# Decay differences of a Mamba-2 scan on GpSimd instead of ScalarE, and the gates of z one step earlier

## The chip, the cores and the metric

The kernel runs on one NeuronCore of a Trainium2 chip, as one launch. The core has a matrix engine (TensorE, PE in the profile), a vector engine (VectorE, DVE), a scalar engine for activation functions (ScalarE, ACT), a general engine (GpSimd, POOL), a queue engine (SyncE, SP) and 16 DMA engines. Each engine works through its own list in order; semaphores tie the lists together. The metric is the time of one execution on the device in microseconds, as the median of several runs: 1495.35 us for three runs of the kernel before (1494.41 to 1498.49).

## What is computed

Two residual layers over 256 tokens of width 1024, all in float32: sliding-window attention with a dense SwiGLU, then a Mamba-2 mixer with a top-2-of-8 expert SwiGLU. The change is in the mixer. Cut to what matters there:

```python
z, xbc, dt = jnp.split(h @ w_in, [D_INNER, D_INNER + D_XBC], axis=-1)
xbc = jax.nn.silu(causal_depthwise_conv(xbc, conv_w, conv_b))
# ssd_chunked_scan: 2 chunks of 128 tokens, 4 groups of 8 heads
a_cs = jnp.cumsum((dt * a).reshape(b, nc, L, G, HG), axis=2)
decay = jnp.exp(jnp.where(causal, a_t[..., :, None] - a_t[..., None, :], -jnp.inf))
cb = jnp.einsum('bclgn,bcsgn->bcgls', cc, bc)
y_diag = jnp.einsum('bcghls,bcsghp->bclghp', cb[:, :, :, None] * decay, xd)
# states carried from chunk to chunk give y_off
y = y_diag + y_off + d_skip * xs
y = rms_norm(y * jax.nn.silu(z), norm_w)
return y @ w_out
```

`decay` is 128 x 128 for each of 32 heads and 2 chunks. The kernel computes the exponential of the difference clipped at zero, min(a_l - a_s, 0), so that nothing overflows above the diagonal; the mask comes with `cb`.

## The kernel before

Weights come from HBM in tiles of 128 x 1024. Each is split into a high part (`w_hi`, ScalarE, L1038) and a low part (`w_lo`, VectorE, L1581), and TensorE makes three products with high and low parts of the activations (L2685, L2686, L2693). Four buffers hold split tiles, so ScalarE and VectorE can be at most four tiles ahead of TensorE.

The mixer's input projection is 40 such tiles, called steps 0 to 39 here, in ten column groups: B, C, then x (groups 2 to 5), then the four groups of z (6 to 9), which end at steps 27, 31, 35 and 39. The output projection follows with 16 tiles. At each step every engine's code calls its own `mixer_steps(i)`, in which the remaining work of the mixer is placed at fixed steps: which step and in which order within it is written out by hand, and this is the order in that engine's list. Beside the projection run the convolution (`convolve` on VectorE, 8 instructions each, L2305 and L2308; its gate `conv_silu` on ScalarE, L1475) and the scan.

The scan has eight units u = 0 to 7, one for each pair of group and chunk. Unit u's parts stand at these steps:

- GpSimd (L2635 to L2639) fetches `acs_in`: the running sums of eight heads, spread over all partitions. The next fetch waits until the differences of this unit are done (`acs_used`).
- ScalarE, `unit_decays` (L1477 to L1495), at step 24 + 2u: eight differences 128 x 128 into `dec` (two buffers by u % 2), then one exponential 128 x 1024. From unit 2 on it waits first for TensorE's products of unit u - 2 (`acc_full`), which read the same buffer.
- VectorE, `unit_in` and `unit_mid` (L2368 to L2388), at step 24 + 2u: x times dt into `xd`; for chunk 0 also `xde` with `end_e`; then `dec` times the masked product `cbm` (L2376).
- TensorE, `unit_out`, at step 25 + 2u: one product with the state and eight with `dec` (L3330 or L3333, L3335).
- VectorE, `unit_out` (L2396 to L2405), at step 28 + 2u: adds them up.

ScalarE's `z_of_group(j)` (L1398 to L1406) applies SiLU to a finished z group, its two token halves one after the other. It stands two steps behind the group's last tile: steps 29, 33, 37 and 41. TensorE's first tile of the next z group uses the same accumulators and waits for it. `gated_by_z` on VectorE (L2416) multiplies with the result. ScalarE loads a function table (ACT_TABLE_LOAD) when the next function isn't in the one loaded: SiLU and Exp are in different ones, while copies, squares and Relu need no load.

After the mixer come a norm, the routing and the experts' tiles.

## Time and profile before

| what | value |
|---|---|
| median of three runs | 1495.35 us (1494.41 to 1498.49) |
| the profiled execution | 1497.73 us |
| its span, first to last instruction | 1495.9 us |
| mean granted TensorE clock | 0.991 |
| TensorE busy | 1437.1 us (96%) |
| VectorE busy | 995.1 us (67%) |
| ScalarE busy | 747.6 us (50%) |
| GpSimd busy | 18.6 us (1%), 27 instructions |
| scan: ScalarE's differences, first to last start | 487.6 to 557.6 us |
| output projection | 573.0 to about 619.5 us |

The profile is of one execution. Busy shares are averages over stages with different limits, so the stage around the change is read by itself: which engine waits there, for whom, and who would be next. PEclk is the clock that TensorE was granted as a share of 2.4 GHz; half of it is its lower level. Instructions overlap a little at their ends, so two starts lie closer than one duration.

### The profile page before, as it was taken

Reading aid. Unit: us, or ns where it says so; the run is one execution under the profiler, and the core shown is the slowest. Engines: PE = TensorE matmul, PEld = TensorE weight load, DVE = VectorE, ACT = ScalarE, POOL = GpSimd, SP = SyncE. Lnnn points to the kernel's source line nnn. Section 1 sums busy time; section 2 is a strip of 40 time slices with the busy share of each in tenths; the row PEclk is TensorE's granted clock in tenths of the full one; section 3 lists DMA queues with packets and bytes.
Section 4 is the critical chain, followed back from the end, with each engine's and each line's share of the span. In section 5 each row is a group of like instructions: output and inputs, shape, how many; then the busy total and the mean of one; then the engine's idle time right before and its main releaser. Section 6 shows DMA issues by size and latency. Waiting matters only on the chain.

```text
span 1495.9 us, 18527 instructions
## 1 busy us (share of the span) xinstructions
PE 1437.1 (96%) x6840; PEld 976.6 (65%) x6840; DVE 995.1 (67%) x1271; ACT 747.6 (50%) x977; POOL 18.6 (1%) x27
## 2 busy tenths in 40 slices
PE   7989999999999899999999999999999989999998
PEld 2835787888789778674666556756465655565573
DVE  2578788888659899764666646765654555655563
ACT  3565544444455896353446445644453444545361
POOL 0000000000000000000100000000000000000000
PEclk9999999999999999999999999999999999999999
DMA  9878698888366545679999999999999999999996
GB/s 361 330 248 292 240 396 303 301 295 301 103 217 185 162 161 204 261 288 409 364 412 406 411 374 416 418 420 420 409 420 413 420 420 418 413 420 414 420 419 247
DMA packets 118201, 506.01 MB, mean 338 GB/s; under 512 B 13779, under 2 KB 16492, under 8 KB 83032
## 3 DMA queue, kind: packets, MB, share of 16 engines
q1 hardware_dynamic: 115640, 496.51, 85.6%
q0 software_dynamic: 2464, 8.24, 1.6%
q8 instruction: 57, 0.93, 0.2%
q14 instruction: 40, 0.33, 0.1%
HBM read 502.52 MB, written 2.32 MB: 337 GB/s over the span
## 4 chain that ended last, share of the span: by engine, by line
PE 74%; DVE 10%; DMA 7%; ACT 6%; issue 3%; SPq 0%; DVEq 0%; ACTq 0%
PE acc L2685 16%; PE acc L2693 16%; PE acc L2686 16%; PE acc L3187 15%; DVE w_lo L1581 3%; ACT w_hi L1038 2%; DVE cv L2308 2%; DMA raw_rest<-in_moe_w_down 1%; DMA raw<-in_moe_w_down 1%; PE xb L3071 1%; DMA mod<-in_moe_w_gu 1%; PE acc L2834 1%; DMA mod<-in_moe_w_down 1%; DMA raw<-in_ada_w 1%; ACT dec L1487 1%
## 5 line engine op out<-in xcount | busy, mean ns | idle before, releaser
L1581 DVE TENSOR_TENSOR w_lo<-raw,w_hi 128x1024 fp32r<-128x1024 f32 x356 | 427.3, 1221 | 136.6 <-ACT w_hi L1038 126.1
L1038 ACT ACTIVATE w_hi<-raw 128x1024 fp32r<-128x1024 f32 x356 | 371.0, 1057 | 249.1 <-PE acc L2693 157.7
L2685 PE MATMUL acc<-w_hi,g_hi 128*128 128x512 f32 x448 | 179.3, 400 | 4.0 <-ACT w_hi L1038 3.9
L2686 PE MATMUL acc<-w_hi,g_lo 128*128 128x512 f32 x448 | 174.8, 390 | 0.0
L2685 PE MATMUL acc<-w_hi,a_hi 128*128 128x512 f32 x384 | 155.4, 405 | 8.5 <-ACT z_s L1404 7.7
L2686 PE MATMUL acc<-w_hi,a_lo 128*128 128x512 f32 x384 | 151.4, 394 | 0.0
L2693 PE MATMUL acc<-w_lo,g_hi 128*128 128x512 f32 x448 | 139.1, 392 | 4.1 <-DVE w_lo L1581 4.1
L3187 PE MATMUL acc<-raw,g_s 128*64 128x512 f32 x592 | 131.6, 594 | 0.5 <-DMA raw<-in_moe_w_gu 0.5
L2693 PE MATMUL acc<-w_lo,a_hi 128*128 128x512 f32 x384 | 119.5, 392 | 0.0
L1581 DVE TENSOR_TENSOR w_lo<-mod,w_hi 128x1024 fp32r<-128x1024 f32 x66 | 78.5, 1221 | 60.0 <-ACT w_hi L1038 58.2
L2685 PEld LDWEIGHTS acc<-w_hi,g_hi 128*128 128x128 f32 x448 | 84.2, 188 | 38.4 <-issue 12.7
L1038 ACT ACTIVATE w_hi<-mod 128x1024 fp32r<-128x1024 f32 x66 | 68.1, 1056 | 63.4 <-PE acc L2693 24.6
L2693 PEld LDWEIGHTS acc<-w_lo,g_hi 128*128 128x128 f32 x448 | 83.4, 188 | 24.9 <-DVE w_lo L1581 7.1
L3187 PEld LDWEIGHTS acc<-raw,g_s 128*64 128x64 f32 x592 | 41.3, 137 | 82.5 <-issue 77.8
L2686 PEld LDWEIGHTS acc<-w_hi,g_lo 128*128 128x128 f32 x448 | 84.2, 188 | 16.2
L2685 PEld LDWEIGHTS acc<-w_hi,a_hi 128*128 128x128 f32 x384 | 73.1, 190 | 27.5 <-ACT z_s L1404 8.1
L2685 PE MATMUL acc<-w_hi,e_hi 128*128 128x512 f32 x216 | 87.8, 406 | 2.5 <-issue 2.1
L2686 PE MATMUL acc<-w_hi,e_lo 128*128 128x512 f32 x216 | 85.3, 395 | 0.0
L2693 PEld LDWEIGHTS acc<-w_lo,a_hi 128*128 128x128 f32 x384 | 72.9, 190 | 16.0
L2686 PEld LDWEIGHTS acc<-w_hi,a_lo 128*128 128x128 f32 x384 | 73.2, 191 | 14.0
L2693 PE MATMUL acc<-w_lo,e_hi 128*128 128x512 f32 x216 | 68.6, 399 | 5.8 <-DVE w_lo L1581 5.7
L1618 DVE SCALAR_TENSOR_TENSOR ada<-raw,cond,ada 128x512 f32<-128x512 f32 x84 | 59.1, 746 | 1.4 <-DMA raw<-in_ada_w 1.4
(417 smaller groups left out, 2057.3 us busy)
## 6 DMA issues: line engine op xcount, KB each, us to landing
raw<-in_moe_w_gu SPq DMA_DIRECT2D x136, 1024.0 KB, 14.8
raw<-in_moe_w_down SPq DMA_DIRECT2D x66, 1024.0 KB, 16.5
raw<-in_ada_w SPq DMA_DIRECT2D x96, 512.0 KB, 6.0
mod<-in_moe_w_gu SPq DMA_DIRECT2D x40, 1024.0 KB, 13.8
raw<-in_ffn_w_gu SPq DMA_DIRECT2D x56, 512.0 KB, 5.9
mod<-in_moe_w_down SPq DMA_DIRECT2D x23, 1024.0 KB, 16.3
raw_more<-in_moe_w_gu SPq DMA_DIRECT2D x22, 1024.0 KB, 14.3
raw<-in_ssm_w_in SPq DMA_DIRECT2D x40, 512.0 KB, 5.0
```

The lines of the kernel that those rows point to most:

```text
L1038: act.activation(w_hi[:, w % SPLIT, :], raw_tile(no), ACT.Copy).then_inc(hi_ready, 1)
L1487: ins = act.activation(dec[:, u % 2, cols], acs_in[:, cols], ACT.Relu, scale=-1.0, bias=acs[:, c, HG * g + i:HG * g + i + 1])
L1581: dve.tensor_tensor(w_lo[:, w % SPLIT, :], raw_tile(no), r32(w_hi[:, w % SPLIT, :]), ALU.subtract).then_inc(raw_used, 1)
L1618: ins = dve.scalar_tensor_tensor(dst, src, cond[:, k:k + 1], dst, ALU.mult, ALU.add)
L2308: ins = dve.scalar_tensor_tensor(cv[:, s % 2, m, :], src, wt, cv[:, s % 2, m, :], ALU.mult, ALU.add)
L2685: pe.matmul(o, l_hi[:, k, rows_], hi[:, col:col + HALF], start=new, stop=False)
L2686: pe.matmul(o, l_lo[:, k, rows_], hi[:, col:col + HALF], start=False, stop=False)
L2693: mm = pe.matmul(o, l_hi[:, k, rows_], lo[:, col:col + HALF], start=False, stop=end)
L2834: mm = pe.matmul(o[j:j + 32, 0:HALF], cond[:, k:k + 1].to_broadcast([P, 32]), raw_tile(no)[:, cols], start=k == 1, stop=k >= KD - 2, skip_ ...
L3071: mm = pe.transpose(b[:, m * P:(m + 1) * P], hidden[:, block_of(m)] if B.mixture else hidden[:, m * P:(m + 1) * P], ident)
L3187: mm = pe.matmul(rows_[at_:at_ + SMALL, :], lhs[:, k, :], raw_tile(no)[:, m * HALF:(m + 1) * HALF], start=k == 0, stop=last, skip_group_ch ...
```

## The change

The differences leave ScalarE. GpSimd computes them itself, directly behind the transfer that brings `acs_in`, with one subtract-and-min instruction a head; it now waits for the running sums (unit 0), for the products of unit u - 2, and for its own transfer. ScalarE keeps the exponential, whose sign changes with the clipped difference, and in unit 0 the exponential of the chunk ends comes ahead of it. ScalarE's gates of z stand one step earlier and ahead of the exponential in their step.

```diff
@@ ScalarE, mixer_steps
                 if i not in DECAYS_FIRST:
                     conv_silu(i)
+                for j in range(SG):
+                    if i == PROJ_END[Z0 + j] + 1:
+                        z_of_group(j)
                 for u in range(NU):
                     if i == unit_in_at(u) + LEAD:
                         unit_decays(u)
                 if i in DECAYS_FIRST:
                     conv_silu(i)
-                for j in range(SG):
-                    if i == PROJ_END[Z0 + j] + 2:
-                        z_of_group(j)
@@ ScalarE, unit_decays
                 if u == 0:
                     act.wait_ge(acs_ready, 1)
-                if u >= 2:
-                    act.wait_ge(acc_full, full_no(u - 2))
-                act.wait_ge(ld_acs, 16 * (u + 1))
-                for i in range(HG):
-                    cols = slice(i * P, (i + 1) * P)
-                    ins = act.activation(dec[:, u % 2, cols], acs_in[:, cols], ACT.Relu, scale=-1.0,
-                                         bias=acs[:, c, HG * g + i:HG * g + i + 1])
-                ins.then_inc(acs_used, 1)
+                    act.activation(end_e[:, :, :], end_e[:, :, :], ACT.Exp).then_inc(acse_ready, 1)
                 act.wait_ge(acs_used, u + 1)
-                if u == 0:
-                    act.activation(end_e[:, :, :], end_e[:, :, :], ACT.Exp).then_inc(acse_ready, 1)
-                act.activation(dec[:, u % 2, :], dec[:, u % 2, :], ACT.Exp, scale=-1.0).then_inc(e_ready, 1)
+                act.activation(dec[:, u % 2, :], dec[:, u % 2, :], ACT.Exp).then_inc(e_ready, 1)
@@ GpSimd, for u, (c, g) in enumerate(SUNITS), behind the transfer
+                if u == 0:
+                    pool.wait_ge(acs_ready, 1)
+                if u >= 2:
+                    pool.wait_ge(acc_full, full_no(u - 2))
+                pool.wait_ge(ld_acs, 16 * (u + 1))
+                for i in range(HG):
+                    cols = slice(i * P, (i + 1) * P)
+                    ins = pool.tensor_scalar(dec[:, u % 2, cols], acs_in[:, cols], acs[:, c, HG * g + i:HG * g + i + 1], 0.0,
+                                             ALU.subtract, ALU.min)
+                ins.then_inc(acs_used, 1)
```

ScalarE's list in step 28, between the convolution's gate (L1475) and the exponential of unit 2 (L1493 before, L1484 now), with what follows it in the list before:

```order
 L1475 ACTIVATE cv<-cv 128x512
-L1487 ACTIVATE dec<-acs_in,acs 128x128 x8
-L1493 ACT_TABLE_LOAD
-L1493 ACTIVATE dec<-dec 128x1024
-L1038 ACTIVATE w_hi<-raw 128x1024
-L1431 ACTIVATE xbc<-xb 128x2x256
+L1404 ACTIVATE z_s<-acc 128x512
+L1406 ACTIVATE z_s<-acc 128x512
+L1484 ACT_TABLE_LOAD
+L1484 ACTIVATE dec<-dec 128x1024
```

The eight differences are gone, and the two halves of the gate of z group 0 stand where they stood, behind the gate that uses the same table.

GpSimd's list before, from the store of the running sums to the store of hm, with the semaphores waited for:

```order
L2633 DMA acs_scratch<-dt_rows 32x2x128 [waits acs_rows]
L2638 DMA acs_in<-acs_scratch 128x1024 [waits st_acs]
L2638 DMA acs_in<-acs_scratch 128x1024 [waits acs_used] x7
L2642 DMA hm_scratch<-hm 128x2x1024 [waits hm_rows,hm_rest]
L2595 DMA token_scratch<-token_rows,slot_at 1536x16 [waits token_ready,place_ready,st_zero,st_hm]
```

And now, for units 1 and 2:

```order
L2629 DMA acs_in<-acs_scratch 128x1024 [waits acs_used]
L2638 TENSOR_SCALAR dec<-acs_in,acs 128x128 [waits ld_acs]
L2638 TENSOR_SCALAR dec<-acs_in,acs 128x128 x7
L2629 DMA acs_in<-acs_scratch 128x1024 [waits acs_used]
L2638 TENSOR_SCALAR dec<-acs_in,acs 128x128 [waits ld_acs,acc_full]
```

Each transfer is followed by the unit's differences, and the next transfer stands behind them.

## Rows read from the trace of the kernel before

**Rows 1.** Busy time by stretch: us, busy us (count) of each engine, PEclk, DMA share, GB/s.
```profile
460.00:470.00 10.00, 10.00 (x86) 10.00 (x85) 9.40 (x20) 5.17 (x7) 0.00 (x0) 1.00 0.72 204
...
505.00:515.00 10.00, 4.40 (x27) 3.47 (x25) 8.67 (x15) 8.28 (x15) 0.53 (x1) 0.91 0.44 152
515.00:525.00 10.00, 9.60 (x36) 7.53 (x36) 9.30 (x17) 8.58 (x17) 0.53 (x1) 0.74 0.50 159
...
580.00:600.00 20.00, 20.00 (x97) 16.69 (x96) 19.93 (x23) 10.13 (x13) 0.00 (x0) 1.00 0.76 305
...
620.00:630.00 10.00, 8.51 (x51) 5.37 (x49) 8.96 (x17) 5.28 (x11) 0.00 (x0) 1.00 0.00 0
...
1300.00:1400.00 100.00, 100.00 (x458) 63.44 (x458) 58.77 (x60) 51.09 (x55) 0.00 (x0) 1.00 1.02 417
```

**Rows 2.** Waits, 485 to 580 us: who waited for whom, total us, times, longest.
```profile
PE acc L2685 <- ACT z_s L1404: 7.7, 2, 6.0
```

**Rows 3.** TensorE's timeline: start, us, engine, line, operation, count, [idle before].
```profile
498.40 1.89 PE L3335 MATMUL acc<-xd,dec 128*128 128x64 f32 x16
...
505.92 0.62 PE L2693 MATMUL acc<-w_lo,a_hi 128*128 128x512 f32 x2
...
508.96 0.44 PE L3322 MATMUL xb<-c_t,b_t 128*128 128x128 f32 x2
515.40 0.80 PE L2685 MATMUL acc<-w_hi,a_hi 128*128 128x512 f32 x1 [6.00 <-ACT z_s L1404]
...
520.42 0.60 PE L2733 MATMUL xb<-square,cv 128*128 128x128 f32 x4
520.78 0.48 PE L2685 MATMUL acc<-w_hi,a_hi 128*128 128x512 f32 x1
...
523.61 1.02 PE L3330 MATMUL acc<-xde,xbc 128*128 128x512 f32 x2
...
547.76 0.61 PE L2693 MATMUL acc<-w_lo,a_hi 128*128 128x512 f32 x2
...
554.34 0.80 PE L2685 MATMUL acc<-w_hi,a_hi 128*128 128x512 f32 x1 [1.73 <-ACT z_s L1404]
...
558.74 0.60 PE L2733 MATMUL xb<-square,xbc 128*128 128x128 f32 x4
...
573.00 0.48 PE L2685 MATMUL acc<-w_hi,y_hi 128*128 128x512 f32 x1
```

**Rows 4.** VectorE: its timeline, then three groups of 500 to 572 us.
```profile
491.71 0.69 DVE L2384 TENSOR_TENSOR xde<-xd,end_e 128x512 f32<-128x512 f32 x1 [2.33 <-ACT end_e L1492]
...
512.11 1.23 DVE L2388 TENSOR_TENSOR dec<-dec,cbm 128x1024 f32<-128x1024 f32 x1 [0.70 <-ACT dec L1493]
...
545.11 1.22 DVE L1581 TENSOR_TENSOR w_lo<-raw,w_hi 128x1024 fp32r<-128x1024 f32 x1
...
569.50 0.69 DVE L1645 TENSOR_TENSOR y_lo<-xb,y_hi 128x512 fp32r<-128x512 f32 x1
...
L1581 DVE TENSOR_TENSOR w_lo<-raw,w_hi 128x1024 fp32r<-128x1024 f32 x15 | 18.3, 1219 | 0.9 <-ACT w_hi L1038 0.6
...
L2405 DVE TENSOR_TENSOR xbc<-xbc,acc 128x512 f32<-128x512 f32 x7 | 4.8, 686 | 0.2
...
L2376 DVE TENSOR_TENSOR cbm<-xb,square 128x128 f32<-128x128 f32 x6 | 1.7, 288 | 0.6 <-DVE cv L2308 0.6
```

**Rows 5.** ScalarE's timeline around step 28.
```profile
507.20 2.44 ACT L1487 ACTIVATE dec<-acs_in,acs 128x128 f32<-128x128 f32 x8
509.66 1.28 ACT L1493 ACT_TABLE_LOAD   x1
510.95 1.06 ACT L1493 ACTIVATE dec<-dec 128x1024 f32<-128x1024 f32 x1
...
514.75 0.60 ACT L1404 ACTIVATE z_s<-acc 128x512 f32<-128x512 f32 x1
```

**Rows 6.** GpSimd: its timeline, and the transfers of acs_in.
```profile
0.26 0.10 POOL L3457 MEMSET const-float32-0.0<- 128x1 f32 x1 [0.26 <-issue]
...
DMA to landing us min/median/max: 4.1/4.4/5.3
```

## The prediction

> **What bounds the kernel now.** I read the chain that ended last first, then the busy time by stretch, then the timelines of the scan. From about 760 us to the end the transfers run without a gap (DMA share 1.02 at 417 GB/s) while TensorE is nearly always busy [rows 1]: that part cannot shrink, but it starts when the part in front lets it. At 620 to 630 us nothing is moved at all, so there the engines set the time and not the transfers [rows 1]. A microsecond won or lost in the scan should therefore arrive at the end, unless something takes it on the way.
>
> In the scan (484 to 582 us) TensorE waits in one place worth naming: for ScalarE's gates of z, 7.7 us in two waits [rows 2]. The first tile of z group 1 (step 28) could start at 508.96 + 0.44 = 509.40 and starts at 515.40; the first of group 3 (step 36) starts at 554.34 after 1.73 us [rows 3]. Both tiles then run long: 515.40 to 520.42 is 5.02 us, 554.34 to 558.74 is 4.40, against 520.78 to 523.61 = 2.83 for an undisturbed tile [rows 3]. In that stretch the granted clock averages 0.91 and later 0.74 of 2.4 GHz, that is, the engine fell to its lower level after standing idle [rows 1]. So the two waits cost 6.00 + 2.19 + 1.73 + 1.57 = 11.5 us. The next candidate stands right behind: VectorE is 9.30 of 10 us busy at 515 to 525, in the middle of a disturbed stretch, and 19.93 of 20 at 580 to 600 [rows 1]. The 0.70 us before its instruction at 512.11 are its last wait for another engine that counts [rows 4].
>
> **The removed instructions on ScalarE.** Eight differences take 2.44 us per unit [rows 5], eight units: 19.5 us leave ScalarE's list. Two table loads of 1.28 us come back (the moved gate now stands between a state or convolution gate and an exponential, and in the new order there are 12 loads where there were 10). Net some 17 us of an engine that isn't itself the bound; what counts is what it lets go sooner.
>
> **The z gate.** Before, the gates of group 0 stand behind the differences, a table load, the exponential, a split and a copy: from 507.20 to 514.75 [rows 5]. Now they stand directly behind the convolution's gate in step 28. They then wait only for step 27's tile, whose last two products start at 505.92 and take 0.62 [rows 3]. The first half is out by then; the second takes 0.6 more [rows 5]: 507.1, ahead of 509.40. The wait of 6.00 us goes, and with it the slow clock: up to 8.2 us at step 28. For group 3 the same working puts the gates ahead of TensorE as well.
>
> **What is late next: VectorE.** It can only come forward by its own waits. The two large ones are 2.33 us for the exponential of the chunk ends (now ahead of everything, because the differences in front of it are gone) and 0.70 for the exponential of unit 2 [rows 4]. The last limits the sum: exponential 2 stands behind the z gates, 507.1 + 1.28 (table) + 1.06 = 509.4, against 512.0 now [rows 5]. VectorE's product of unit 2 moves from 512.11 to about 509.5 [rows 4]: 2.6 us earlier, and all behind it by the same, since it runs solid. TensorE can use only that plus the lead that VectorE has over it. The leads: at step 35 the low part is out at 545.11 + 1.22 = 546.33 and is wanted at 547.76, 1.43 us; at the start of the output projection y_lo is out at 569.50 + 0.69 = 570.19 and is wanted at 573.00, 2.81 us [rows 3, 4]. At step 35 TensorE can be 1.43 + 2.6 = 4.0 us early; the second z wait and its slow clock (3.3 us) lie behind it, so this gives 7.3 at step 40; there y_lo allows 2.81 + 2.6 = 5.4. The last number is the ceiling: **5.4 us**, not 11.5.
>
> **The added work on GpSimd.** It issues eight differences per unit behind each transfer, and holds the next transfer until they are done; nothing else is queued there but hm's store, wanted after 620. Transfers land in 4.4 us [rows 6]. For unit u it waits for the products of unit u-2: for unit 2 these start at 498.40 and take 1.89 [rows 3], so it has from 500.3 to about 508.4 before ScalarE's exponential stands still. For units 5 and 7 the time allowed is 11.7 and 9.7 us, for unit 3 10.4 (each: VectorE's product at its new time, less 1.06 for the exponential, less the end of the products two units back). What one GpSimd difference takes no row shows. Lower end: the 128x1 memset, 0.10 us. Upper end of the nearest kind: ScalarE's same difference, 2.44 / 8 = 0.305, and VectorE's 128x128 product, 0.288 [rows 4 to 6]. Eight at 0.305 are 2.4 us: hidden everywhere.
>
> **What GpSimd takes from VectorE.** This is the term that decides. Of the 72 us from 500 to 572, VectorE works some 70, and only about 14 of them lie in the seven groups that read PSUM or one tensor; the rest read two tensors from SBUF (one group of either kind is shown, with the 128x128 product) [rows 4]. If a GpSimd instruction that reads SBUF holds off a VectorE one, 48 of them (units 2 to 7) fall into the stretch where VectorE is solid, some 80% = 38 against such a reader. The price of one collision lies between 0 and 0.305 us: 0 to 11.6 us in all. I take 0.11, near the memset's length, the only compute row of this engine: VectorE has small gaps of its own (some 0.2 us, as behind each convolution) where a read can hide. 38 x 0.11 = 4.2 us. Units 0 and 1 fall to 457 to 470 us, where TensorE is solid and VectorE 9.40 of 10 busy [rows 1]: I cost them at nothing; uncovered they would be 16 x 0.11 = 1.8 us.
>
> **The sum.** -5.4 + 4.2 = -1.2 us. The profiled execution took 1497.73 (span 1495.9 and 1.8 around it), 2.4 above the median of the three runs, 1495.35; so it would come to 1496.5 and the median to **1494.1 us**.
>
> **The rivals.**
> *The port is free.* VectorE loses nothing: -5.4, 1490.0 us. For it: the differences are short, and nothing in this profile shows GpSimd disturbing VectorE. Against: it never computed here. 27%.
> *GpSimd holds VectorE off for its whole length.* The place is VectorE's list from 500 to 570, the price 0.305 x 38 = 11.6, the result +6.2: 1501.5 us. It turns the change into a loss from 5.4 / 38 = 0.14 us per collision. For it: VectorE's work there is four fifths two-tensor reads. Against: the gaps. 25%. The Trainium skill ("SBUF — State Buffer", who interferes with whom) states just such a rule: a VectorE instruction with two SBUF inputs and a GpSimd one that reads SBUF exclude each other, and the second to issue blocks fully. No run here shows it yet. For the price, the skill ("GPSIMD Engine Reference", performance versus the Vector engine) gives 1.8 cycles an element at 1.2 GHz, an estimate of 0.19 us for 128 elements; by that the sum would be -5.4 + 7.2 = +1.8 us.
> *GpSimd itself is too slow.* From 9.7 us per unit (1.2 us an instruction, which could also come from being held off by VectorE) ScalarE waits for the differences, and behind it the splits. At 1.6 us an instruction (12.8 us a unit) it is some 3 us over for units 3, 5 and 7: +9 - 5.4 = +3.6, 1499.0 us. 8%.
> *The gain doesn't arrive.* The transfers of the expert part swallow it: 0, 1495.3 us. Against: 620 to 630 us without any transfer. 8%.
> My forecast itself: 32%.
>
> **Range and chances.** 0.3% is 4.5 us, about what a measurement of this kernel tells from no change. Faster by more needs a free port and little lost to short waits (a short stall can itself bring the slow clock, as 1.73 us did at step 36): most of the first rival, 28% with the edge of the forecast. Slower by more: most of the second and third, 29%. Between: 43%. The range leaves out the tail beyond 0.2 us per collision and a half: 1489.0 to 1502.5 us.
>
> **What the profile of the changed kernel would show.** That the z step is right: no TensorE wait for z_s above 1 us, granted clock near 1 at 505 to 525. That VectorE is next: TensorE waits for w_lo at steps 31 to 35 and for y_lo at the start of the output projection. The port: VectorE's 128x1024 subtractions longer than 1.22 us, or pauses before them, only while GpSimd works; if they stay at 1.22 the first rival holds. GpSimd's speed: the distance between starts of its differences. If the exponential of units 3 to 7 waits for dec from GpSimd, the third rival holds. I am wrong if the wait for z stays, if TensorE is over 5.4 us early at the first tile of the output projection, or if the shift there isn't the shift at the end.

## The result and the profile after

| | median | runs | profiled execution, its span |
|---|---|---|---|
| before | 1495.95 us | 1494.41 to 1498.49 (4) | 1497.73, 1495.9 us |
| changed | 1504.2 us | 1502.42 to 1506.05 (4) | 1502.42, 1500.6 us |

The ratio is 1.0054, 95% interval 1.0034 to 1.0073: slower, by 8 us in the medians, and outside the range of the prediction. (The two profiled executions lie only 4.7 us apart: that of before is one of its slower runs, that of the changed kernel its fastest.) The first tile of the output projection starts at 578.49 instead of 573.00, 5.5 us late, so the loss is made in the scan.

The waits of the scan come first, since [rows 2] had its answer there. From 485 to 590 us (engine, line, waited for: us in total, times, longest):

```profile
ACT dec L1484 <- POOL dec L2638: 22.8, 6, 8.2
POOL dec L2638 <- DMA acs_in<-acs_scratch: 16.6, 5, 3.5
...
DVE dec L2379 <- ACT dec L1484: 7.6, 5, 2.5
...
PE xb L2734 <- ACT xbc L1431: 6.3, 2, 4.0
```

The wait for z is gone. In its place stands a chain: TensorE's transposition (`xb<-square,cv`) waits for ScalarE's copy of x (`xbc`), VectorE for ScalarE's exponential, ScalarE for GpSimd's differences (22.8 us in six waits), GpSimd for its transfer. GpSimd's timeline shows why:

```profile
499.56 8.31 POOL L2638 TENSOR_SCALAR dec<-acs_in,acs 128x128 f32<-128x128 f32 x8 [18.66 <-PE acc L3336]
508.17 0.58 POOL L2629 DMA_DIRECT2D acs_in<-acs_scratch  x1 [0.30 <-POOL dec L2638]
511.92 7.84 POOL L2638 TENSOR_SCALAR dec<-acs_in,acs 128x128 f32<-128x128 f32 x8 [3.17 <-DMA acs_in<-acs_scratch]
...
560.81 7.66 POOL L2638 TENSOR_SCALAR dec<-acs_in,acs 128x128 f32<-128x128 f32 x8 [3.18 <-DMA acs_in<-acs_scratch]
```

In units 2 to 7 eight differences take 7.66 to 8.56 us, about 1.0 us each, not 0.3. Then 0.30 us to the issue, 0.58 for it, 3.2 to 3.5 until the data are there, and only then the next eight: there is one `acs_in`. From unit 2 to unit 7 the starts lie (560.81 - 499.56) / 5 = 12.25 us apart. TensorE needs much less. Where it doesn't wait (e5 below), its products of one unit and the next start at

```profile
516.77 1.89 PE L3341 MATMUL acc<-xd,dec 128*128 128x64 f32 x16
...
525.58 1.89 PE L3341 MATMUL acc<-xd,dec 128*128 128x64 f32 x16
```

8.8 us apart. GpSimd falls behind by 3.4 us a unit. ScalarE's timeline of the changed kernel, answering [rows 5]:

```profile
504.70 0.58 ACT L1404 ACTIVATE z_s<-acc 128x512 f32<-128x512 f32 x1
505.70 0.60 ACT L1406 ACTIVATE z_s<-acc 128x512 f32<-128x512 f32 x1 [0.43 <-PE acc L2694]
506.32 1.28 ACT L1484 ACT_TABLE_LOAD   x1
507.90 1.06 ACT L1484 ACTIVATE dec<-dec 128x1024 f32<-128x1024 f32 x1 [0.30 <-POOL dec L2638]
...
519.79 1.06 ACT L1484 ACTIVATE dec<-dec 128x1024 f32<-128x1024 f32 x1 [3.06 <-POOL dec L2638]
520.75 1.04 ACT L1038 ACTIVATE w_hi<-raw 128x1024 fp32r<-128x1024 f32 x1
521.70 0.58 ACT L1431 ACTIVATE xbc<-xb 128x512 f32<-128x512 f32 x1
```

In step 28 all is as forecast: the second half of z is out at 506.3 and the exponential 3.05 us sooner than in [rows 5]. Of these, 0.87 us are from ahead of the scan, whose first product starts at 484.09 in this execution and at 484.96 in that of before; the change itself gives 2.2. One unit later the exponential waits, and the split and the copy of x behind it wait too. TensorE's timeline, answering [rows 3], shows who needed them:

```profile
522.42 0.71 PE L2734 MATMUL xb<-square,cv 128*128 128x128 f32 x4 [2.31 <-ACT xbc L1431]
536.98 1.09 PE L2734 MATMUL xb<-square,cv 128*128 128x128 f32 x4 [3.95 <-ACT xbc L1431]
...
559.46 0.50 PE L2686 MATMUL acc<-w_hi,a_hi 128*128 128x512 f32 x1 [2.33 <-ACT w_hi L1038]
...
578.49 0.47 PE L2686 MATMUL acc<-w_hi,y_hi 128*128 128x512 f32 x1 [1.10 <-DVE y_lo L1636]
```

And by stretch, with the columns of [rows 1]:

```profile
505.00:515.00 10.00, 10.00 (x53) 8.05 (x53) 9.48 (x16) 7.08 (x9) 6.54 (x8) 1.00 0.45 157
515.00:525.00 10.00, 7.68 (x40) 6.29 (x39) 8.86 (x14) 6.37 (x10) 6.29 (x8) 0.89 0.32 110
...
535.00:545.00 10.00, 8.02 (x39) 6.74 (x40) 7.31 (x9) 4.29 (x7) 8.56 (x8) 0.83 0.33 111
```

The stretch of the old z wait is full now (10.00 busy, clock 1.00, against 4.40 and 0.91). The loss lies behind it, where every engine but GpSimd stands: VectorE, 9.50 busy before at 535 to 545, has 7.31.

The lengths of VectorE's own instructions hardly suffer. The group from 485 to 572 us that lost most in total (mean ns of one behind the comma), before and then changed:

```profile
L2308 DVE SCALAR_TENSOR_TENSOR cv<-u_pad,vecs,cv 128x256 f32<-128x256 f32 x18 | 7.4, 478 | 0.0
```

```profile
L2299 DVE SCALAR_TENSOR_TENSOR cv<-u_pad,vecs,cv 128x256 f32<-128x256 f32 x18 | 8.0, 509 | 0.0
```

This group, `xbc<-xbc,srow` (684 and then 745 ns) and the five groups with smaller differences (`w_lo`, the other convolution, `raw` and the two scalings, 9 to 41 ns a piece) come to 1.6 us over 48 instructions of GpSimd, 0.03 us each. VectorE's own loss is in its waits for the exponential, 7.6 us in the list above.

### The profile page after: what moved, and what is told of

Same layout as the page of the kernel before. It is cut to its first block, busy times and chain, and to the rows that moved or that the text cites. A ratio compares the mean times of both kernels' runs of the same rounds, so it can differ in the third digit from the quotient of the medians.

```text
span 1500.6 us, 18531 instructions
## 1 busy us (share of the span) xinstructions
PE 1436.4 (96%) x6840; PEld 974.1 (65%) x6840; DVE 996.8 (66%) x1271; ACT 731.3 (49%) x915; POOL 84.6 (6%) x91
## 4 chain that ended last, share of the span: by engine, by line
PE 76%; DMA 9%; DVE 7%; POOL 3%; ACT 3%; issue 2%; SPq 0%; DVEq 0%; ACTq 0%; POOLq 0%
PE acc L2686 16%; PE acc L2694 16%; PE acc L2687 15%; PE acc L3188 15%; POOL dec L2638 3%; DVE w_lo L1572 3%; DMA raw_rest<-in_moe_w_down 1%; DMA mod<-in_moe_w_gu 1%; DMA raw<-in_moe_w_down 1%; PE xb L3072 1%; DMA acs_in<-acs_scratch 1%; PE acc L2835 1%; DMA raw<-in_moe_w_gu 1%; ACT w_hi L1038 1%; DMA mod<-in_moe_w_down 1%
## 5 line engine op out<-in xcount | busy, mean ns | idle before, releaser
L2638 POOL TENSOR_SCALAR dec<-acs_in,acs 128x128 f32<-128x128 f32 x64 | 65.6, 1040 | 44.7 <-DMA acs_in<-acs_scratch 26.0
```

The costliest lines, as they stand in the source:

```text
L2638: ins = pool.tensor_scalar(dec[:, u % 2, cols], acs_in[:, cols], acs[:, c, HG * g + i:HG * g + i + 1], 0.0, ALU.subtract, ALU.min)
```

## The experiments

Theory 1 at the start: GpSimd's loop is too slow. Its rivals: the early z gates cost by themselves, or GpSimd's work costs VectorE time. The medians, and, as the yardstick in the trace, the way from TensorE's first product of unit 0 (`xb<-c_t,b_t` near 484 us) to the first tile of the output projection. The way is one execution each and free of what varies ahead of the scan; before and e4, whose lists are the same up to there, both have 88.04.

| kernel | median us | ratio, 95% interval | way us |
|---|---|---|---|
| before | 1495 to 1496.8 | 1 | 88.04 |
| changed | 1504.2 | 1.0054 [1.0034, 1.0073] | 94.40 |
| e1 z gates early, all on ScalarE | 1500.21 | 1.0037 [1.0023, 1.0050] | 91.80 |
| e2 GpSimd alone, z as before | 1505.43 | 1.0072 [1.0058, 1.0086] | 97.39 |
| e3 changed, two buffers | 1495.1 | 0.9995 [0.9986, 1.0004] | 86.56 |
| e4 before, with a probe on GpSimd | 1496.77, one run | | 88.04 |
| e5 differences ahead of conv gate | 1491.03 | 0.9969 [0.9959, 0.9980] | 83.74 |
| e6 e5, z group 0 early | 1492.66 | 0.9977 [0.9967, 0.9986] | 84.06 |
| e7 e6, even units on GpSimd | 1499.23 | 1.0030 [1.0016, 1.0044] | 89.87 |
| e8 e5, all z gates early | 1495.6 | 1.0004 [0.9995, 1.0014] | 87.27 |
| e9 changed, in place | 1505.7 | 1.0066 [1.0041, 1.0092] | 95.90 |
| e10 e9, z nearly as before | 1505.51 | 1.0056 [1.0036, 1.0077] | 97.54 |
| e11 e5, z group 1 early | 1493.7 | 0.9981 [0.9971, 0.9991] | 85.03 |
| e12 e11, squares one step later | 1491.15 | 0.9968 [0.9955, 0.9982] | 82.34 |
| e13 e8, four of eight on GpSimd | 1494.6 | 0.9989 [0.9979, 0.9998] | 85.69 |
| e14 e12, four of eight on GpSimd | 1491.33 | 0.9970 [0.9957, 0.9982] | 83.56 |

### The two parts apart: e1 and e2

e1 is the kernel before with only this:

```diff
                 if i not in DECAYS_FIRST:
                     conv_silu(i)
+                for j in range(SG):
+                    if i == PROJ_END[Z0 + j] + 1:
+                        z_of_group(j)
...
-                for j in range(SG):
-                    if i == PROJ_END[Z0 + j] + 2:
-                        z_of_group(j)
```

> The kernel before with the z gates alone moved one step up; the differences stay on ScalarE. Theory A (GpSimd's loop of transfer, eight differences and next transfer, 12 us a unit through one buffer, is what cost the time; the z part is sound): the wait of 6.0 us for z at step 28 and the slow clock behind it go, but VectorE doesn't come forward, since the exponential of unit 2 still stands behind the differences. TensorE can then use only VectorE's leads, 1.4 us at step 35 and 2.8 at the first tile of the output projection: -2.8 us. Theory B (moving z in front of the exponentials delays the exponentials and with them VectorE): 0 to +2 us, and VectorE waits for exponentials after step 28.

Measured +5 us, above both theories. No wait for z is left, but its waits from 485 to 590 us are:

```profile
PE xb L2733 <- ACT xbc L1431: 8.1, 3, 3.8
...
DVE dec L2388 <- ACT dec L1493: 4.8, 4, 2.4
DVE w_lo L1581 <- ACT w_hi L1038: 3.3, 4, 2.2
```

So moving the z gates is a loss by itself: 7.7 us of waits for z turned into 8.1 us of waits for the copy of x, and VectorE waits more. What stands behind the gate now, the differences, a load, the exponential, a split, a copy, is what TensorE and VectorE need next. Theory B has the direction, and sees only VectorE in it.

e2 is the changed kernel with the z gates back at their old places (that diff reversed).

> The changed kernel with the z gates at their old place: only the differences move to GpSimd. Theory A (one buffer in series): GpSimd's starts stay 12 us apart for units 2 to 7, and the time is the changed kernel's or slightly above it, +8 to +11 us on before. Theory B (the z gates ahead of the exponential are what delays): near before, -2 to +2 us, and the starts on GpSimd are further apart only where the products come late.

```profile
ACT dec L1484 <- POOL dec L2638: 29.0, 6, 7.6
...
PE acc L2686 <- ACT z_s L1404: 14.8, 3, 6.5
```

Measured +10 us (1505.43 against 1495.05). ScalarE waits for GpSimd as in the changed kernel, and with z behind it TensorE waits for z three times and longer than ever. That is theory A. Each part alone loses, and they don't add up (5 and 10 against 8). With the differences on GpSimd the early gates cost nothing more: 1.2 us less in the median, where the intervals overlap, and 3.0 us less on the way. So the 5 us of e1 are no part of the changed kernel's 8.

### GpSimd's loop and its price: e3 and e4

e3 gives the transfers a second buffer, so that GpSimd fetches unit u + 2 while it works on u + 1:

```diff
+            fetch(0)
+            fetch(1)
             for u, (c, g) in enumerate(SUNITS):
...
-                pool.wait_ge(ld_acs, 16 * (u + 1))
+                pool.wait_ge(ld_two[u % 2], 16 * (u // 2 + 1))
...
+                if u + 2 < NU:
+                    pool.wait_ge(acs_used, u + 1)
+                    fetch(u + 2)
```

> The changed kernel with a second buffer for acs_in in a free slot of the modulation rows and one semaphore for each: the transfer of unit u + 2 runs under the differences of unit u + 1. Theory A (series of transfer and differences): the 4.1 us between the end of one unit's differences and the start of the next go, the eight differences alone are 8.3 us against 8.8 us for TensorE's pitch of a unit, ScalarE's waits for GpSimd shrink from 22.8 us to under 5, and the time is below before: -5.4 + about 2 for VectorE's lengthened instructions = -3 us. Theory C (the shared port: what costs is that VectorE and GpSimd hold each other off): VectorE's instructions and GpSimd's stay as long, and the time stays above before by at least 3 us.

```profile
499.42 9.28 POOL L2642 TENSOR_SCALAR dec<-acs_in,acs 128x128 f32<-128x128 f32 x8 [24.37 <-PE acc L3343]
...
509.62 9.15 POOL L2642 TENSOR_SCALAR dec<-acs_in_b,acs 128x128 f32<-128x128 f32 x8
...
551.13 9.36 POOL L2642 TENSOR_SCALAR dec<-acs_in_b,acs 128x128 f32<-128x128 f32 x8
```

The period falls to (551.13 - 499.42) / 5 = 10.3 us, and the time by 9 us: taking the transfer out of the series gives back what the changed kernel had lost against the kernel before. It gives no more. Theory A had expected 3 us below before and under 5 us of waits of ScalarE for GpSimd; the time is that of before, and the waits are 12.7 us in five. GpSimd pauses only once for TensorE, 0.86 us, and still misses 8.8: its eight take 8.0 to 11.2 us, 9.4 in the mean. Theory C's 3 us above before are ruled out too. In the same order of the z gates e3 is 5 us below e1 (1495.1 against 1500.21): there GpSimd's work, fetched ahead, is the better choice.

e4 is the kernel before, with like instructions of GpSimd put into two places (they write `dec`, which nobody reads by then; `flat` is `dec` as one row, `tri` a constant; a few more take a number instead of the column, one of them at 128x512): behind the scan, where VectorE is solid (it works without a pause), and at 611 us, where it waits.

```diff
+                for m in range(n):
+                    pool.tensor_scalar(flat[:, m * P:(m + 1) * P], tri, column[:, 5:6], 0.0, ALU.subtract, ALU.min)
...
+            pool.wait_ge(y_ready, NU)
+            probe(8, 2)
+            pool.wait_ge(token_ready, 1)
+            probe(4, 1)
```

> The kernel before; GpSimd additionally runs difference instructions on constants into the unused dec buffers: eight 128x128 with a scalar from memory, two 128x128 with an immediate scalar and one 128x512 with an immediate, once from about 579 us, where VectorE is solid, and four, one and one from about 612 us, where VectorE stands idle for 5.7 us. Theory C (the shared port makes GpSimd's instruction long): about 1.0 us each under the solid VectorE and 0.3 or less in the idle stretch. Theory D (the instruction itself costs GpSimd 1 us, whatever VectorE does): about 1.0 in both. The immediate forms and the 128x512 tell whether the cost is one of the instruction or of its elements.

```profile
578.12 14.69 POOL L2644 TENSOR_SCALAR dec<-square 128x128 f32<-128x128 f32 x8 [28.64 <-DVE xbc L2417]
592.88 2.39 POOL L2646 TENSOR_SCALAR dec<-square 128x128 f32<-128x128 f32 x2
...
611.67 2.79 POOL L2644 TENSOR_SCALAR dec<-square 128x128 f32<-128x128 f32 x4 [13.88 <-DVEq L2455]
614.53 0.64 POOL L2646 TENSOR_SCALAR dec<-square 128x128 f32<-128x128 f32 x1
615.24 1.92 POOL L2647 TENSOR_SCALAR dec<-square 128x512 f32<-128x512 f32 x1
```

One 128x128 instruction takes 2.79 / 4 = 0.70 us beside an idle VectorE and 14.69 / 8 = 1.84 us beside a solid one: neither theory C's 0.3 nor theory D's 1.0 in both places. ScalarE is idle in the fast place too, so e4 alone can't say which of the two engines holds GpSimd off. The transfers don't: their share is 1.03 in the fast place and 0.63 in the slow one. e13 below has four at 0.70 us beside a busy ScalarE (1.90 of 2.79 us), while three of VectorE's four instructions read or write `acc`, in PSUM:

```profile
515.55 2.79 POOL L2662 TENSOR_SCALAR dec<-acs_in,acs 128x128 f32<-128x128 f32 x4 [2.71 <-PE acc L3360]
```

That points to VectorE, and to its instructions with all inputs in SBUF, as far as one place can. VectorE, over the stretch with eleven of GpSimd's (ten of 128x128, one of 128x512), needs 18.60 us from one `w_lo` to a later one, for what takes 17.97 without: 0.06 each. But 0.40 of these 0.63 us are in one instruction, beside the 128x512 one, that takes 1.62 us instead of 1.22:

```profile
595.92 1.62 DVE L1582 TENSOR_TENSOR w_lo<-raw,w_hi 128x1024 fp32r<-128x1024 f32 x1
```

So beside ten short instructions of 128x128 GpSimd is held off and VectorE hardly at all (0.23 us, an estimate from the rest); beside the one long one VectorE is held off too.

### The order of ScalarE's list: e5, e6, e8, e11, e12

In the kernel before ScalarE stands 2.93, 2.44 and 0.79 us for the convolution with the differences right behind. The second, in step 28:

```profile
506.67 0.63 ACT L1475 ACTIVATE cv<-cv 128x512 f32<-128x512 f32 x1 [2.44 <-DVEq L2314]
```

e5 puts them in front, and leaves everything else as it was before:

```diff
+                for u in range(NU):
+                    if i == unit_in_at(u) + LEAD:
+                        unit_differences(u)
                 if i not in DECAYS_FIRST:
                     conv_silu(i)
```

> The kernel before with one change: in each step ScalarE does its eight differences ahead of the convolution's gate instead of behind it; the gates of z stay where they were, GpSimd does nothing new. Theory 1 (what decides is the order of ScalarE's list in step 28 and its neighbours, since ScalarE stands still for the convolution there, 2.4 and 0.8 us, while the differences could run): the exponential, the split and the z gate come up to 2.4 us sooner, the wait of TensorE for z at step 28 shrinks from 6.0 to about 3.5 us, and the time falls by 2 to 4 us: 1491 to 1493. Theory 2 (the differences wait for the products two units back and for their transfer, so ahead of the convolution's gate they only pass their wait on to it): VectorE's and TensorE's waits for the gate appear, the time is 1495 to 1498.

```profile
509.85 0.50 PE L2691 MATMUL acc<-w_hi,a_hi 128*128 128x512 f32 x1 [1.33 <-ACT z_s L1404]
531.16 0.79 PE L2691 MATMUL acc<-w_hi,a_hi 128*128 128x512 f32 x1 [3.41 <-ACT z_s L1404]
```

Faster by 4.6 us (0.9969), with no instruction added or removed, as theory 1 had it (1491 to 1493). The wait for z at step 28 falls from 6.00 to 1.33 us, more than the 2.4 expected; a new one of 3.41 comes at step 32.

e6 adds the early gate for z group 0 alone, e8 for all four groups:

> As the run before, and in addition the gates of z of group 0 alone one step up, in step 28 directly behind the convolution's gate (they share its table of functions, no load is added); groups 1 to 3 stay. Theory 1 (a z gate moved up is good where TensorE stands still for it for 6 us and where no load comes with it; moving all four groups cost 5 us because of what stands behind them): the wait of 6.0 us and the slow clock behind it go, the way from unit 0's first product to the output projection is 83 to 85 us instead of 88.0, the time 1490 to 1492. Theory 2 (any z gate in front of exponential, split and copy costs elsewhere what it gives here): TensorE waits 2 to 4 us for the copy of x or the split instead, the time is 1494 to 1498.

> The kernel before with the differences ahead of the convolution's gate, and the z gates of all four groups one step up; nothing on GpSimd. The z gates alone one step up took 1500.2 (+5 us). Theory 1 (they cost by what stands behind them: 2.4 us of differences are now in front of the gate instead, in ScalarE's idle time): TensorE's waits for the copy of x shrink from 8.1 us to about half, the time is 1495 to 1498. Theory 2 (they cost by the two added table loads and the lost lead of one step, whatever stands behind): 1499 to 1501, as without the move.

e6 loses the wait at step 28 and gets one of 1.28 us for `w_lo` and 3.97 for z at step 32: no gain over e5 (0.9977 against 0.9969). That is theory 2's claim, that such a gate costs elsewhere what it gives here; the time, 1492.66, lies between the ranges of the two. e8 is back at the time of before. Theory 1 of that run has its numbers: the time is in its range, and the waits for the copy of x are about halved, from 8.1 us in e1 to this one:

```profile
533.61 0.63 PE L2739 MATMUL xb<-square,cv 128*128 128x128 f32 x4 [3.90 <-ACT xbc L1431]
```

Its cause isn't borne out by that. In e5's order, too, the z gates all one step up cost 4.6 us, the same as in the old order (5 us): what e8 has over e1 is e5's own gain. So the differences behind the gates were not what made these dear.

e11 moves only group 1's gate, into step 32 behind the convolution's gate, and e12 also the squares:

```diff
-                    if i == PROJ_END[Z0 + j] + 2:
+                    if i == PROJ_END[Z0 + j] + 2 - (j == 1):
...
-                    if i == PROJ_END[Z0 + u // 2] + 4 + u % 2:
+                    if i == PROJ_END[Z0 + u // 2] + 4 + u % 2 + (u < 6):
```

> The kernel with the differences on ScalarE ahead of the convolution's gate (1491.0 us), and the z gate of group 1 one step sooner directly behind the convolution's gate. In that kernel TensorE stood 3.41 us for this gate at 527.75 to 531.16 and ran the next tile at the slow clock (5.25 us from its start to the next x piece). Theory 1: the wait shrinks by what now stands between the two places (a square, a split and a copy, 2.0 us) to 1.4 us, -2 to -4 us: 1487 to 1489. Theory 2 (what is put behind the gate, the split and the copy, is waited for in its place): 1490 to 1492.

> As the run before, and in addition the squares of y for units 0 to 5 one step later on ScalarE, since it stands 2.9, 2.7 and 2.4 us for them while differences behind them could run. Theory 1 (ScalarE's in-order waits are what delays its gates and splits): the wait for z of group 1 goes, VectorE or the split's low part is next, another -1 to -3 us: 1485 to 1488. Theory 2 (VectorE is the bound by now, 93% busy at 515 to 545): the same time as the run before within 1 us.

e11 missed both its ranges: 1493.7, its way 1.3 us longer than e5's. Its trace shows where. The wait of 3.41 us is down to 1.36, but the clock falls behind it all the same, and group 3's gate now makes TensorE wait:

```profile
528.84 0.50 PE L2691 MATMUL acc<-w_hi,a_hi 128*128 128x512 f32 x1 [1.36 <-ACT z_s L1404]
...
550.17 0.80 PE L2691 MATMUL acc<-w_hi,a_hi 128*128 128x512 f32 x1 [2.32 <-ACT z_s L1404]
```

The tiles behind the two take 4.46 and 4.40 us instead of 2.83, so waits and slow clock come to 6.9 us, against 3.41 and a tile of 5.25 us, 5.8 in all, in e5. That is 1.1 of the 1.3 us. e12 missed its ranges as well (1485 to 1488, or e11's time within 1 us): it is 2.5 us below e11. It has the shortest way of all, 82.34 us; its time can't be told from e5's. What bounds it then can be read from its waits and stretches:

```profile
532.67 0.73 PE L2699 MATMUL acc<-w_lo,a_hi 128*128 128x512 f32 x2 [1.19 <-DVE w_lo L1587]
542.12 0.73 PE L2699 MATMUL acc<-w_lo,a_hi 128*128 128x512 f32 x2 [0.84 <-DVE w_lo L1587]
...
566.03 0.47 PE L2691 MATMUL acc<-w_hi,y_hi 128*128 128x512 f32 x1 [1.01 <-DVE y_lo L1651]
```

```profile
525.00:535.00 10.00, 8.81 (x48) 7.02 (x47) 9.39 (x12) 9.97 (x21) 0.53 (x1) 1.00 0.38 127
```

VectorE is 9.3 to 9.5 of 10 busy from 505 to 555 us, and TensorE waits for it 2.5 us for `w_lo` and 1.0 for `y_lo`, at the places that the prediction named, with the clock at 1.00 (the columns of [rows 1]). One wait for z is left, 1.33 us at step 28. From 573.00 the first tile of the output projection comes to 566.03, and the span falls by 7.3 us with it: what is won in the scan arrives. (These are two executions; in the medians it is 4.8 us, the ratio 0.9968.)

### GpSimd with a shorter list: e7, e9, e10, e13, e14

e7 gives GpSimd only the even units (two buffers, e6's order):

```diff
+                if u % 2 == 0:
+                    return
...
-                act.wait_ge(ld_acs, 16 * (u + 1))
+                act.wait_ge(ld_two[1], 16 * (u // 2 + 1))
```

> As the run before, and in addition two buffers for the transfers, and the differences of units 0, 2, 4 and 6 on GpSimd, those of units 1, 3, 5 and 7 still on ScalarE. GpSimd has 17.6 us for each of its units then and needs 8 to 10, so by theory 1 (the added work was bad only by its serial loop) ScalarE waits for it under 1 us, loses 9.8 us of work, and the time is that of the run before or up to 2 us less: 1489 to 1491. By theory 2 (GpSimd's work costs by what it takes from VectorE, 32 instructions by 0.06 to 0.3 us) it is 2 to 8 us above the run before.

```profile
539.15 9.88 POOL L2660 TENSOR_SCALAR dec<-acs_in,acs 128x128 f32<-128x128 f32 x8 [4.39 <-PE acc L3361]
```

```profile
549.06 1.06 ACT L1503 ACTIVATE dec<-dec 128x1024 f32<-128x1024 f32 x1 [4.52 <-POOL dec L2660]
```

Half the work, and 6.6 us slower than e6. Theory 1 failed, since the period isn't all; the 6.6 us lie in theory 2's range, but its cause, time taken from VectorE, is not where the trace has the largest wait. GpSimd may start unit 6 only at 539.15, when the products of unit 4 have read `dec`; from there to the exponential it needs 9.9 us where ScalarE needs 2.4. Behind that exponential stands z's gate, and TensorE waits for it 5.01 us. So the length of the eight in a row counts too, once the way from one use of `dec` to the next is tight. (TensorE's waits for `w_lo` grow as well, from 1.3 to 2.6 us.)

e9 was to free GpSimd of that as well: differences in place in `acs_in`, two buffers, the exponential writes `dec`.

```diff
+                    ins = pool.tensor_scalar(acs_two[u % 2][:, cols], acs_two[u % 2][:, cols], acs[:, c, HG * g + i:HG * g + i + 1], 0.0,
+                                             ALU.subtract, ALU.min)
+                ins.then_inc(acs_used, 1)
+                if 1 <= u < NU - 1:
+                    pool.wait_ge(e_ready, u)
+                    fetch(u + 1)
```

> The changed kernel with GpSimd's loop opened: two buffers for the transfers, and the differences written in place in them instead of into dec, so that GpSimd waits for no product of TensorE and works up to two units ahead; ScalarE's exponential reads the buffer, writes dec and takes over the wait for the products two units back. The 64 differences on GpSimd and the order of the z gates stay as changed. Theory 1 (the changed kernel lost by the latency of GpSimd's loop: transfer, then differences of some 8 us, tied to the products two units back): ScalarE's wait for GpSimd goes, and the time falls from 1504 to 1490 to 1493, below the kernel before, since ScalarE is rid of 19.5 us of work. Theory 2 (the 64 instructions cost VectorE their length, and the early z gates cost by themselves as they did alone): 1497 to 1501, TensorE waiting for w_lo and for the copy of x.

> GpSimd's opened loop as in the run before, but the z gates at their old places, save that of group 1, which comes one step sooner directly behind the convolution's gate (same table of functions, no load added): 10 loads as before. Theory 1: without the differences ScalarE reaches every z gate 2.4 us sooner or more, so none of TensorE's waits for z above 1 us is left, VectorE bounds the scan: 1487 to 1490. Theory 2 (GpSimd's instructions cost VectorE): 2 to 5 us above the same order without GpSimd, that is 1491 to 1494.

```profile
509.23 9.07 POOL L2641 TENSOR_SCALAR acs_in_b<-acs_in_b,acs 128x128 f32<-128x128 f32 x8 [4.20 <-DMA acs_in_b<-acs_scratch]
518.25 0.59 POOL L2631 DMA_DIRECT2D acs_in<-acs_scratch  x1
523.11 8.00 POOL L2641 TENSOR_SCALAR acs_in<-acs_in,acs 128x128 f32<-128x128 f32 x8 [4.27 <-DMA acs_in<-acs_scratch]
```

The edit did not do what it was for. The fetch of unit u + 1 stands behind the differences of unit u in GpSimd's list, so transfer and differences are in series again, with a period of 13.1 us (e10: 13.2), and both kernels are as slow as the changed one or slower, outside the ranges of both theories. Unmeant, they extend the series over the period: 10.3, 12.2, 13.1 us give ways of 86.6, 94.4, 95.9 us in the same order of z.

That left open whether GpSimd's work costs anything once it keeps up. e13 (e8's order) and e14 (e12's order) share each unit: four differences on GpSimd, four on ScalarE, the exponential in two halves, two buffers.

```diff
-                for i in range(HG):
+                for i in range(HG // 2, HG):
                     cols = slice(i * P, (i + 1) * P)
...
-                act.activation(dec[:, u % 2, :], dec[:, u % 2, :], ACT.Exp, scale=-1.0).then_inc(e_ready, 1)
+                act.activation(dec[:, u % 2, HALF:2 * HALF], dec[:, u % 2, HALF:2 * HALF], ACT.Exp, scale=-1.0)
+                act.wait_ge(diffs_down, u + 1)
+                act.activation(dec[:, u % 2, 0:HALF], dec[:, u % 2, 0:HALF], ACT.Exp).then_inc(e_ready, 1)
```

> The z gates all one step up as in the changed kernel, two buffers for the transfers, and the eight differences of each unit shared: four on GpSimd, four on ScalarE ahead of the convolution's gate; the exponential in two halves. In the runs so far the starts of GpSimd's differences lay 12.2 us apart in the changed kernel, 13.1 and 13.2 in two variants whose transfer still stood behind the differences, and 10.3 with two buffers, and the times were 1504, 1506, 1506 and 1495. Theory 1 (GpSimd's period against TensorE's 8.8 us a unit is the whole loss): four differences take 4 to 5 us, GpSimd keeps up, ScalarE waits for it under 1 us in all, and the time is at or below the same order without GpSimd (1495.6): 1492 to 1495. Theory 2 (each instruction on GpSimd also costs VectorE): 32 instructions, 0.06 to 0.3 us each, 1497 to 1503.

> The best order so far (all differences on ScalarE ahead of the convolution's gate, the z gate of group 1 one step up, squares of y one step later: 1491.15 us) with the same sharing: four differences of each unit on GpSimd, four on ScalarE. Theory 1: GpSimd keeps up and disturbs little, but VectorE already bounds (TensorE waits 2.5 us for its low parts), so the time is the same within 1.5 us: 1490 to 1492.5. Theory 2: GpSimd's 32 instructions lengthen a VectorE that bounds: 1493 to 1500.

GpSimd now mostly waits for TensorE instead of the reverse. In e14:

```profile
517.05 5.11 POOL L2662 TENSOR_SCALAR dec<-acs_in,acs 128x128 f32<-128x128 f32 x4 [4.84 <-PE acc L3360]
```

e13 takes 1494.6 (0.9989) against 1495.6 (1.0004) of the same order without GpSimd, e14 1491.33 (0.9970) against 1491.15 (0.9968): the intervals overlap in both pairs, barely in the first. Both times are in the range of theory 1 and outside that of theory 2. But ScalarE still waits for GpSimd, once for 1.8 us in e13, where theory 1 allowed under 1, and three times in e14:

```profile
ACT dec L1502 <- POOL dec L2662: 7.3, 3, 3.5
```

The ways are 1.6 us shorter than e8's and 1.2 us longer than e12's. So the difference is at most a microsecond or two either way, and its sign isn't shown. What leaves ScalarE (9.8 us of differences, less 1.5 for the exponential in two halves) gains no more than that. In e14 VectorE bounds by then: TensorE waits 3.5 us for its `w_lo`, 2.5 in e12.

## Why the prediction was wrong

It said 1494.1 (1489.0 to 1502.5) and gave slower 29%; the time is 1504.2.

**The removed instructions and the z gate (its own view of step 28): right there.** The wait of 6.00 us and the slow clock went, the exponential of unit 2 came out 3.05 us sooner. 2.6 was forecast for VectorE; it has 509.07 against 512.11, of which 0.87 is from ahead of the scan, so 2.2.

**"Eight at 0.305 are 2.4 us: hidden everywhere": this step failed first.** The price came from the two engines whose like instructions the trace showed, and its upper end was 0.305 us. GpSimd needs 0.70 alone (e4), 0.96 to 1.07 in the changed kernel's units 2 to 7. The trace of before had no row of GpSimd computing, so the upper end was no bound at all: the nearest row belonged to another engine.

**The allowance was computed for the wrong thing.** The prediction says that the transfer is held until the differences are done and that it lands in 4.4 us, and then compares the differences alone with the 9.7 to 11.7 us between products and exponential. In series the loop is 0.3 + 0.6 + 3.3 + 8.0 = 12.2 us against 8.8 for a unit on TensorE. That condition breaks at (8.8 - 4.2) / 8 = 0.57 us an instruction, not at the 1.2 us that it gave. This is the point from which GpSimd is no longer hidden, not yet the one from which the change loses: e3 has a period of 10.3 us and the time of before. A cautious price, three times a neighbour's, gives 8 x 0.92 + 4.2 = 11.5 us, between e3's period and the changed kernel's: a loss of some microseconds. e3 shows the term: without the transfer in the loop 9 us come back.

**The third rival had the mechanism and only 8%.** It looked for 1.6 us an instruction and 1499.0 us; 1.0 us an instruction was enough for 1504.2, by the series above. Its sum is off as well: 12.8 us against the allowances that it gives itself, 10.4, 11.7 and 9.7, is 2.4 + 1.1 + 3.1 = 6.6 us over, not 9.

**The z gates as a pure gain: wrong.** The prediction worked out when z would be ready and what VectorE gains, and took the engines behind the gate as served. e1 measures +5 us for this part alone; beside GpSimd's work (changed kernel against e2) it gives 1.2 us within the noise, where up to 8.2 were forecast at step 28. Under "What is late next" the answer given was VectorE; it was ScalarE's own list, above all the copy of x that TensorE transposes (8.1 us of waits in e1, 6.3 in the changed kernel), and e8 finds the same 4.6 us in another order.

**What GpSimd takes from VectorE: mis-sized.** 0.11 us each were put in, 4.2 us in all; measured 0.03 (changed kernel) to 0.06 (e4, 0.02 without the long one). So the term of which the prediction says that it decides was some 1.6 us. The second rival had the direction reversed: VectorE holds GpSimd off, 1.84 us against 0.70. The rule of the Trainium skill ("SBUF — State Buffer", who interferes with whom), that the two exclude each other and the second to issue blocks, fits GpSimd's side; on VectorE's side these runs show it beside the one instruction of 128x512 (1.62 us against 1.22) and almost none of it beside those of 128x128.

**VectorE as the next bound, and the shift that arrives at the end: borne out, but in another kernel.** The changed kernel never got there. e12 did, with the differences on ScalarE and the squares moved: its way is 88.04 - 82.34 = 5.7 us shorter, TensorE waits for `w_lo` and `y_lo`, and it arrives in the time. That this is near the 5.4 us of the prediction is partly luck, since they were worked out for other lists; whether 5.4 would have been the changed kernel's ceiling no run shows.

What stays open: which part of e8's 4.6 us is the two added loads and which the lost lead, and why 1.36 us of waiting brought the slow clock in e11 and 1.33 us, at step 28 of the same kernel, did not. A version that keeps GpSimd clear of both loops with all eight differences was not built.

## What to carry to other kernels

Before work goes to an engine that the trace has never seen compute, add up its whole loop, transfer and issue included, and compare the period with that of the consumer; then ask from what price per instruction it breaks, and treat a neighbour's duration as no bound. Before a gate is moved forward in an in-order list, write down who waits for each instruction that it passes. The cheap gain here lay in neither: work that was ready was put in front of a wait in the same list (-4.6 us with nothing added).

## What the runs showed of the hardware

- GpSimd, subtract and min, float32, beside an idle VectorE: for 128x128 0.70 us by a column operand and 0.64 by a number, for 128x512 1.92 us by a number. The last two differ by 1.28 / 384 = 3.3 ns an element. The Trainium skill ("GPSIMD Engine Reference", performance versus the Vector engine) has 1.8 cycles an element at best, an estimate of 0.77 us for 512; this form took over twice that, and the measurement decides.
- The form with a column, at 128x128, takes 1.84 us while VectorE is solid (e4), and in the scan 0.93 to 1.40 us each in rows of eight (e7, e3), 0.70 to 1.81 in rows of four (both in e13). VectorE lost 0.03 to 0.06 us per instruction.
- In e4 a solid VectorE cost GpSimd about the same for each instruction by a number, whatever its length: 1.20 us against 0.64 for 128x128, 2.45 against 1.92 for 128x512. By a column it was 1.1 us more. The long instruction is also the one that cost VectorE 0.40 us.
- A stall of one microsecond can cost 1.6 more through the clock, or nothing. At the start of the output projection TensorE waits 1.10 us for `y_lo` in e3 and 1.01 in e12. It isn't this small difference: the changed kernel waits 1.10 us there too and keeps its clock (its projection takes 46.38 us). In e3 the clock falls behind it and the projection takes 47.95 us, in e12 it stays and takes 46.36, like before. The rows, 570 to 580 us, e3 and then e12 (the clock is the third number from the end; 0.83 is a stretch in part at the lower level, 0.5):

```profile
570.00:580.00 10.00, 9.49 (x39) 7.79 (x40) 9.50 (x12) 5.67 (x9) 0.00 (x0) 0.83 0.42 142
```

```profile
570.00:580.00 10.00, 10.00 (x46) 8.29 (x45) 9.75 (x13) 6.55 (x12) 0.00 (x0) 1.00 0.42 120
```
